# Moving columns of the float32r matmuls read in turns, four from each half, in a fused two-block kernel

## What is computed

```python
h = rmsnorm(x, g_mix)
z = h @ w_in                                   # 1024 -> 4608
a = silu(layernorm(causal_dwconv(a_val * sigmoid(a_gt), 31 taps)))
s = sc_b * causal_dwconv(sc_c * sc_v, 3 taps)
x = x + (g_a * (a @ w_a_out) + g_b * (s @ w_b_out)) @ w_o
f = gelu(causal_dwconv(h @ w_up_1, 3 taps)) * (h @ w_up_2)     # 1024 -> 2 x 2816
x = x + f @ w_down
x = rmsnorm(x + sigmoid(rmsnorm(x) @ w_ple_gate) * (p @ w_ple))
# second block
q, k, v = rms_norm(x) @ w_in_2                 # 1024 -> 2304
mix = windowed attention with sinks (8 heads), differential attention (4 heads)
x = x + rms_norm(mix @ w_out_2)
g, val = causal_dwconv(rms_norm(x) @ w_up_2, 3 taps)           # 1024 -> 2 x 4096
out = x + rms_norm((gelu(g) * val) @ w_down_2)
```

## Time and profile before

| | |
|---|---|
| median of 3 runs | 752.45 us (752.36 to 752.64) |
| profiled execution | 752.84 us |
| its span | 750.8 us |
| granted TensorE clock, mean | 1.000 |
| PE busy | 743.0 us (99%), 5950 matmuls |
| PE weight loads busy | 722.7 us (96%) |
| VectorE busy | 578.7 us (77%) |
| ScalarE busy | 452.0 us (60%) |
| GpSimd busy | 210.6 us (28%) |
| moved by DMA | 135.48 MB, mean 180 GB/s |

### The profile page before, as it was taken

The page is one execution under the profiler, slowest core; times in us unless marked ns, Lnnn a source line. Parts: engine busy times, 40 slices in busy tenths (PEclk is TensorE's granted clock), DMA queues, the critical chain, the costliest instruction groups (busy, mean ns, idle before and its releaser), DMA issues.

```text
span 750.8 us, 16764 instructions
## 1 busy us (share of the span) xinstructions
PE 743.0 (99%) x5950; PEld 722.7 (96%) x5950; DVE 578.7 (77%) x1049; ACT 452.0 (60%) x765; POOL 210.6 (28%) x136
## 2 busy tenths in 40 slices
PE   9999999999999999999999999999999999999997
PEld 9999999999999999999999999999999999988885
DVE  6899986877887887434987794799999999973333
ACT  7645456556665665445765798876766666643431
POOL 0477642460000000343464003322112212212220
PEclk9999999999999999999999999999999999999999
DMA  8566553565555567544444344365555555666551
GB/s 307 182 217 205 184 166 127 197 201 195 194 180 189 190 204 250 198 162 152 159 161 139 115 134 125 111 199 200 192 190 195 180 184 196 210 212 193 186 179 56
DMA packets 37917, 135.48 MB, mean 180 GB/s; under 512 B 4464, under 2 KB 4720, under 8 KB 37872
## 3 DMA queue, kind: packets, MB, share of 16 engines
q1 hardware_dynamic: 37728, 134.86, 54.4%
q10 hardware_dynamic: 144, 0.00, 0.0%
HBM read 133.80 MB, written 1.05 MB: 180 GB/s over the span
## 4 chain that ended last, share of the span: by engine, by line
PE 89%; DVE 3%; ACT 3%; issue 2%; POOL 1%; DMA 1%; SPq 0%; DVEq 0%; POOLq 0%; ACTq 0%
PE bank L1901 25%; PE bank L1902 25%; PE bank L1903 25%; PE bank L2349 4%; PE bank L2348 4%; PE bank L2347 4%; DVE w_lo L1223 1%; ACT w_hi L787 1%; DMA raw<-in_w_in 1%; POOL X L755 1%; PE bank L2176 1%; ACT score L1079 0%; PE bank L2200 0%; PE bank L1959 0%; DVE sumsq L1813 0%
## 5 line engine op out<-in xcount | busy, mean ns | idle before, releaser
L1901 PE MATMUL bank<-h_hi,w_hi 128*128 128x256 f32 x1372 | 385.9, 281 | 0.3 <-DVE w_lo L1223 0.2
L1902 PE MATMUL bank<-h_lo,w_hi 128*128 128x256 f32 x1372 | 382.9, 279 | 0.0
L1903 PE MATMUL bank<-h_hi,w_lo 128*128 128x256 f32 x1372 | 382.8, 279 | 0.0
L787 ACT ACTIVATE w_hi<-raw 128x1024 fp32r<-128x1024 f32 (+2 forms) x243 | 258.9, 1068 | 93.2 <-PE bank L1903 41.3
L1223 DVE TENSOR_TENSOR w_lo<-raw,w_hi 128x1024 fp32r<-128x1024 f32 (+2 forms) x187 | 236.6, 1268 | 85.9 <-ACT w_hi L787 84.0
L1901 PEld LDWEIGHTS bank<-h_hi,w_hi 128*128 128x128 f32 x1372 | 257.9, 188 | 1.8 <-DVE w_lo L1223 0.7
L1902 PEld LDWEIGHTS bank<-h_lo,w_hi 128*128 128x128 f32 x1372 | 258.0, 188 | 0.0
L1903 PEld LDWEIGHTS bank<-h_hi,w_lo 128*128 128x128 f32 x1372 | 257.9, 188 | 0.0
L636 POOL TENSOR_TENSOR w_lo<-raw,w_hi 128x1024 fp32r<-128x1024 f32 (+1 forms) x56 | 139.0, 2485 | 382.9 <-ACT w_hi L787 374.7
L1281 DVE TENSOR_TENSOR bank<-bank,scales 128x256 f32<-128x256 f32 x116 | 49.5, 430 | 26.3 <-PE bank L1903 17.6
L1572 DVE SCALAR_TENSOR_TENSOR cg<-bank,vec,cg 128x255 f32<-128x255 f32 x108 | 51.5, 476 | 0.7 <-ACT cg L1019 0.6
(11 more groups left out here) (235 smaller groups left out, 963.2 us busy)
## 6 DMA issues: line engine op xcount, KB each, us to landing
raw<-in_w_up SPq DMA_DIRECT2D x108, 512.0 KB, 3.3
raw<-in_w_in SPq DMA_DIRECT2D x53, 512.0 KB, 3.4
raw<-in_w_down SPq DMA_DIRECT2D x32, 512.0 KB, 4.2
raw<-in_w_down SPq DMA_DIRECT2D x16, 704.0 KB, 4.2
raw<-in_w_o SPq DMA_DIRECT2D x8, 512.0 KB, 4.3
raw<-in_w_gate SPq DMA_DIRECT2D x8, 512.0 KB, 3.4
raw<-in_w_out SPq DMA_DIRECT2D x8, 512.0 KB, 3.3
raw<-in_w_b_out SPq DMA_DIRECT2D x4, 512.0 KB, 3.6
```

The lines of the kernel that those rows point to most:

```text
L787: nc.scalar.activation(hi_of(u)[:, cols], raw[s][:, cols], ACT.Copy).then_inc(hi_ready, 1)
L1901: nc.tensor.matmul(ps, wh, hi[:, k, :], start=start and n == 0, stop=False)
L1902: nc.tensor.matmul(ps, wh, lo[:, k, :], start=False, stop=False)
L1903: last = nc.tensor.matmul(ps, wl, hi[:, k, :], start=False, stop=stop and n == len(ks) - 1)
```

## The change

A helper `in_turns` gives a view of columns in which four columns of the first half come first, then four of the second half, then the next four of the first half, and so on. The moving operand and the PSUM output of every float32r matmul get that view: 256 token columns (halves of 128 columns, 512 bytes apart) in `products`, `lagging` and `rounded_first`, 512 weight columns (halves of 256 columns, 1024 bytes apart) in `token_products`. Each product still lands at the address at which it landed before, since input and output are walked in the same order. The stationary operands, the transposes, the attention's score and value products and all the other engines' instructions are as they were. No instruction is added, removed or moved on any engine: the access patterns of the matmuls alone differ, 32x2x4 in place of 256 columns and 64x2x4 in place of 512.

```diff
+            def in_turns(columns):
+
+                return columns.rearrange("p (b i e) -> p i b e", b=2, e=4)
+
             def products(ps, s, block0, ks, hi, lo, start, stop, ready=None, w=None):
 
+                ps = in_turns(ps)
                 w_of = w or (w_hi[s], w_lo[s])
...
-                    nc.tensor.matmul(ps, wh, hi[:, k, :], start=start and n == 0, stop=False)
-                    nc.tensor.matmul(ps, wh, lo[:, k, :], start=False, stop=False)
-                    last = nc.tensor.matmul(ps, wl, hi[:, k, :], start=False,
+                    x_hi, x_lo = in_turns(hi[:, k, :]), in_turns(lo[:, k, :])
+                    nc.tensor.matmul(ps, wh, x_hi, start=start and n == 0, stop=False)
+                    nc.tensor.matmul(ps, wh, x_lo, start=False, stop=False)
+                    last = nc.tensor.matmul(ps, wl, x_hi, start=False,
...
-                            nc.tensor.matmul(ps, wh, hi[:, k, :], start=start and k == ks[0], stop=False)
-                            nc.tensor.matmul(ps, wl, hi[:, k, :], start=False, stop=False)
+                            x_hi = in_turns(hi[:, k, :])
+                            nc.tensor.matmul(in_turns(ps), wh, x_hi, start=start and k == ks[0], stop=False)
+                            nc.tensor.matmul(in_turns(ps), wl, x_hi, start=False, stop=False)
...
-                to, tok = o_tile(half, b)[:], slice(b * P, (b + 1) * P)
+                to, tok = in_turns(o_tile(half, b)[:]), slice(b * P, (b + 1) * P)
                 cols = slice(first_col(u) + j * HALF, first_col(u) + (j + 1) * HALF)
-                wh, wl = (w[slot(u)][:, cols] for w in (w_hi, w_lo))
+                wh, wl = (in_turns(w[slot(u)][:, cols]) for w in (w_hi, w_lo))
```

More of the change, by code:

```diff
@@ L1919, in lagging @@
                         for ps, s in tiles:
-                            last = nc.tensor.matmul(ps, w_hi[s][:, behind * P:(behind + 1) * P],
-                                                    lo[:, behind, :], start=False,
+                            last = nc.tensor.matmul(in_turns(ps), w_hi[s][:, behind * P:(behind + 1) * P],
+                                                    in_turns(lo[:, behind, :]), start=False,
                                                     stop=stop and k is None)
@@ L2012, in rounded_first @@
             def rounded_first(u):
-                ps = in_tile(u)
+                ps = in_turns(in_tile(u))
                 for k in range(DC):
                     wh = w_hi[slot(u)][:, k * P:(k + 1) * P]
-                    nc.tensor.matmul(ps, wh, h2_hi[:, k, :], start=k == 0, stop=False)
-                    nc.tensor.matmul(ps, wh, h2_lo[:, k, :], start=False, stop=False)
+                    nc.tensor.matmul(ps, wh, in_turns(h2_hi[:, k, :]), start=k == 0, stop=False)
+                    nc.tensor.matmul(ps, wh, in_turns(h2_lo[:, k, :]), start=False, stop=False)
                 unit_here(u)
                 for k in range(DC):
-                    last = nc.tensor.matmul(ps, w_lo[slot(u)][:, k * P:(k + 1) * P], h2_hi[:, k, :],
-                                            start=False, stop=k == DC - 1)
+                    last = nc.tensor.matmul(ps, w_lo[slot(u)][:, k * P:(k + 1) * P],
+                                            in_turns(h2_hi[:, k, :]), start=False, stop=k == DC - 1)
                 last.then_inc(unit_done, 1)
```

## The result

| | before | after |
|---|---|---|
| median of the runs | 752.42 us (752.36 to 752.64, 4 runs) | 810.81 us (810.64 to 810.86, 4 runs) |
| span of the profiled execution | 750.8 us | 808.6 us |

The change makes the kernel 58.4 us slower: a ratio of 1.0775, 95% interval 1.0756 to 1.0794. I had said 726 us, with a range of 710 to 745. The sign is wrong, and the result is outside the range by 66 us.

What follows compares the result with a forecast made beforehand. The prediction took TensorE's pitch from one matmul start to the next as the bound. Savings of 0.3 + 3.0 + 3.5 + 11 + 2.1 + 4.2 + 2.8 = 26.9 us from 752.84 gave 726 us, range 710 to 745.

Steps and rivals of the forecast that it cites:

- The views read first: Profile reading: TensorE busy 743.0 of 750.8 us, clock 1.00; distance between matmul starts (116.7 ns at 256 columns) is the measure.
- 6.7 ns are left over: Each matmul's pitch beyond 0.430 ns a column: 116.7 against 110.0 at 256 columns, 226.7 against 220.0 at 512.
- nothing changes: Rival: the 6.7 ns belong to the change from one matmul to the next, not the two reads; 752.5 us, chance 0.07.
- a PSUM write at zero: Matmul output: writing PSUM in four-column runs was taken to cost zero, though no row showed it.
- Bounds of the saving: Moving read of each changed matmul: between nothing and all 6.7 ns saved; 6.7 taken, new pitches 110 and 220.
- The argument beside it: Moving read: both halves, 512 or 1024 bytes apart, lie in the same place of any small memory pattern.
- The two reads that meet: SBUF: the moving read runs at twice the weight load's speed and must pass it repeatedly; placement costs 3.3 to 6.7 ns.
- reads in step: In turns, each half of the moving read advances at the load's speed and never meets it, saving 6.7 ns a matmul.
- The slow rival: PSUM write of every changed matmul: new output runs cost time, some 880 us or, at a smaller price, 768; chance 0.12.
- VectorE as the cap: Stages 20 to 100 and 485 to 655 us: nearly full VectorE limits the gains to 3.0 and 4.2 us.
- The stall behind GpSimd: Second up projection: one `f_lo` takes 1.74 us instead of 0.42 during a GpSimd subtraction; faster TensorE doesn't remove it.
- The signs: Pitches to look for afterwards: near 110 ns as forecast, 113 partial gain, 117 nothing, over 120 slower; transposes still at 109.

Runs made afterwards that it cites:

- read_only: The change with only the moving operand read in turns and the PSUM output written in order: 810.83 us.
- streams4: The change with runs of four columns taken from four parts in turns (256 bytes apart at 256 columns, 512 at 512) instead of two: 852.94 us.
- past0: The change with RING_PAST = 0, so that weights and moving tiles lie at the same place modulo 128 bytes: 811.64 us.
- near64_past0: near64 with RING_PAST = 0, the ring buffers placed 32 bytes further on: 750.64 us.
- map_start64: Kernel before; second down projection only: columns in turns from parts 64 bytes apart, each unit's moving read starting 16 bytes further on: 753.2 us.
- write_only: The change with the moving operand read in order and only the PSUM output written in turns: 752.74 us.
- near64: The change with four-column runs from parts 64 bytes apart at both widths (16 and 32 parts): 744.2 us, ratio 0.988 to the kernel before.

## Why the prediction was wrong

**The views read first** were read rightly: TensorE led, the clock was 1.00, the busy share said nothing, and the pitch times the number of matmuls gives the result (61.1 us for 57.8). But one step there says less than it seems to. The 0.430 ns a column is the difference of two pitches, 116.7 and 226.7, so that the same 6.7 ns are left over at both widths by the arithmetic alone. It was counted as evidence twice, for the rival "nothing changes" and for a PSUM write at zero, and it is none for either.

**The step that failed** is "Bounds of the saving: nothing at the one end, all of the 6.7 ns that are left over at the other", of the moving read. I had bounded an unknown price from one side alone: the moving read's own 0.430 ns a column came from reads in order, and I took it to hold whatever the address order, so that a loss could come from PSUM only. read_only shows the whole +10.0 and +23.3 ns to be this read's. Whether it would be paid without a load beside it isn't shown: no kernel here has turns without loads.

**The argument beside it** made it worse: "both halves lie 512 or 1024 bytes from each other, in the same place of any small pattern". I had this as harmless. The table shows reads that follow each other at 128 bytes and more to be the dear ones, 256 bytes the dearest, and 64 bytes free.

**The two reads that meet.** The reckoning of the left-over doesn't carry over to turns, since the halves lie 512 bytes apart at the one width and 1024 at the other. With 512 bytes at both widths (streams4 for 512 columns) the pitches are 126.7 and 268.0, and from them the left-over would be below zero. What the runs do show is that the weights' place, worth 3.3 ns in order, is worth nothing in the change (past0) and 1.7 ns with 64-byte turns (near64_past0). That fits the idea that reads in step don't disturb each other, but doesn't show it: a read slowed by itself may simply leave room. The full 6.7 ns were reached over one whole unit alone, of `map_start64` at 512 columns (220.2 ns, start 208), with turns 64 bytes apart and not those of the change. At 256 columns 114.7 is the best pitch of a whole stage, 113.3 of a unit. So 220 can be had, and why at that place stays open.

**The PSUM write at zero** was right (write_only). The slow rival, at 0.12, had the right sign, from the wrong place. Its two prices, 768 and 880 us, enclose the result by accident: at 0.16 ns a run it would have fitted 256 columns, but write_only has 0.00.

**VectorE as the cap** of two stages never came into play, because TensorE became slower. The stall behind GpSimd is still there (one `f_lo` of 1.52 us at 607.44), and costs nothing. near64 doesn't test the cap: from the transposes of `X` to the second down projection it needs 183.7 us for 186.5, 2.8 less, where 1536 matmuls at 2.0 ns would give 3.1 and my cap allowed 4.2.

**The signs** I had listed did their work: "over 120 the slow one" was met by 126.7, the transposes stayed, and the pitch didn't follow the number of runs. The chances did not: 0.81 on faster rested on a mechanism that no row showed, with its only loss in another memory, the PSUM. An access pattern that no row shows should have had a loss of its own as a rival, since the pitches of the earlier trace rows already said that addresses matter to this read.

## What to carry to other kernels

Price a new access pattern on the read and the write side apart, and let each of the two unknowns lose as well as gain; a rate measured on reads in order says nothing of another order. With 5232 matmuls under one change, one nanosecond of pitch is 5 us: so one look at the pitch with the pattern on one side alone, then at two or three distances, decides before anything is built on it. Here turns of four floats 64 bytes apart gained 1.2%, and the same turns 256 and 512 bytes apart lost 13% (852.94 against 754.17).

## What the runs showed of the hardware

- A moving read in runs of four floats depends on the distance of the runs: at 256 columns -2 ns for 64 bytes, +7 for 128, +16.7 for 256, +10 for 512; at 512 columns 0, +20, +51 and +41, +23.3 for 1024. With two parts at 512 columns, 13 ns and more are paid at each of ten distances from 1024 to 1408 bytes, and 7 to 10 more at 1024 and 1280, and at 1040, where the way back is 1024.
- Runs of two floats cost 56.6 ns at 256 columns, runs of 16 floats 3.3, runs of 64 nothing (parts 512 bytes apart).
- The PSUM output in 16-byte runs, 64 or 128 of them a matmul, costs nothing: 116.8 and 227.3 ns.
- In order, the place of the moving read against the weights is worth 113.3 to 120.0 ns at 256 columns and 227.4 to 234.9 at 512. With turns 64 bytes apart it is 113.4 to 118.1 and 220.2 to 230.0.
- The place of the weights alone moves the pitch too: 116.7 and 120.0 ns in order, 114.9 and 116.6 in turns 64 bytes apart. The Trainium skill ("TensorE: Matmul & The Clock Gate", "Step-by-step: what each phase is for") has two independent read ports, and no read bandwidth taken by the load; these pitches don't agree with it, whatever the mechanism is.
